# A hybrid trunk step: the work between the RWKV scans in three strips, moved between engines, and begun earlier

## The reference

```
def centred_shift(p, mu_prev, mu_next):
    ...
    return p + mu_prev * (p_prev - p) + mu_next * (p_next - p)

kkf = heads((k * k_k).astype(jnp.float32))
kk = kkf * lax.rsqrt(jnp.sum(kkf * kkf, axis=-1, keepdims=True) + 1e-12)
g = jax.nn.sigmoid(glo) @ g_up
for d, rev in enumerate((False, True)):
    w_log = -softplus(-(w0[d] + tanh(wlo) @ w_up[d])) - 0.5
    decay = exp(-exp(w_log))
    a = sigmoid(a0[d] + alo @ a_up[d])
    kd = k * (1 + (a - 1) * k_a)
    y, s_fin = rwkv_scan(r, decay, kd, v, kk, a, s0[:, d], rev)
    ...
yf = ys[0] + ys[1]
mu = mean(yf); var = mean(square(yf - mu))          # over the 64 of a head
y = (yf - mu) * rsqrt(var + GN_EPS) * gn_g + gn_b
y = y + (bonuses[0] + bonuses[1]) * v
return y * g, finals
```

## Time and profile before

| what | us |
|---|---|
| median of 3 runs | 3958.61 |
| lowest, highest | 3956.07, 3959.44 |
| the profiled execution | 3956.13 |
| its span | 3954.4 |
| TensorE busy in it | 3578.8 (91%) |
| VectorE busy in it | 1311.3 (33%) |
| mean granted TensorE clock | 0.953 |

### The profile page before, as it was taken

One profiled execution on the slowest core, in us unless ns is written; L12 is line 12 of the kernel. 1 busy time (PEld: TensorE's weight loads), 2 busy tenths in 40 slices (PEclk: granted clock), 3 DMA queues, 4 the chain that ended last, 5 costly groups with the idle time before them and its releaser, 6 DMA issues. The chain is left out here.

```text
span 3954.4 us, 81654 instructions
## 1 busy us (share of the span) xinstructions
PE 3578.8 (91%) x36990; PEld 3118.8 (79%) x36990; DVE 1311.3 (33%) x3130; ACT 650.1 (16%) x1649; POOL 189.7 (5%) x150
## 2 busy tenths in 40 slices
PE   5979798897979988739999999999999999999995
PEld 2467494775935554439999999999999999999995
DVE  3476777767634443451111111111111111111112
ACT  2222323222214452200000000000000000000001
POOL 0000101001010000000000000000000000000000
PEclk7989899998989989869999999999999999999997
DMA  7200000000031103149878787877878787878772
GB/s 315 59 8 12 12 4 20 3 16 12 4 89 30 30 2 112 70 149 347 267 262 268 261 273 264 268 264 267 270 267 267 266 271 261 269 262 268 262 262 107
DMA packets 498248, 664.33 MB, mean 168 GB/s; under 512 B 31134, under 2 KB 436950, under 8 KB 494830
## 3 DMA queue, kind: packets, MB, share of 16 engines
q1 hardware_dynamic: 492094, 640.18, 48.3%
q0 software_dynamic: 5632, 18.88, 1.8%
q10 hardware_dynamic: 176, 0.05, 0.0%
HBM read 630.70 MB, written 28.36 MB: 167 GB/s over the span
## 5 line engine op out<-in xcount | busy, mean ns | idle before, releaser
L1990 PE MATMUL bank<-e_hid,e_wd 128*128 128x144 f32 x5632 | 760.1, 288 | 0.0
L1978 PE MATMUL bank<-e_xT,e_wg 128*128 128x144 f32 x5632 | 749.5, 286 | 1.0 <-ACT e_xT L2032 1.0
L1978 PE MATMUL bank<-e_xT,e_wu 128*128 128x144 f32 x5632 | 748.2, 286 | 0.0
L2075 DVE TENSOR_TENSOR e_tm<-bank,e_sg 128x144 f32<-128x144 f32 x352 | 108.4, 308 | 1852.9 <-ACT e_sg L2039 1852.9
L1978 PEld LDWEIGHTS bank<-e_xT,e_wg 128*128 128x128 f32 x5632 | 715.5, 190 | 1.0 <-issue 1.0
L1990 PEld LDWEIGHTS bank<-e_hid,e_wd 128*128 128x128 f32 x5632 | 710.5, 190 | 5.6
L1978 PEld LDWEIGHTS bank<-e_xT,e_wu 128*128 128x128 f32 x5632 | 714.5, 190 | 0.0
L2039 ACT ACTIVATE e_sg<-bank 128x144 f32<-128x144 f32 x352 | 102.5, 291 | 1998.2 <-PE bank L1978 1998.2
L519 PE MATMUL bank<-hT_x,wblk 128*128 128x512 f32 (+1 forms) x672 | 237.2, 512 | 10.0 <-DMA wblk<-in_w_in 8.6
L519 PEld LDWEIGHTS bank<-hT_x,wblk 128*128 128x128 f32 x672 | 115.6, 199 | 125.0 <-issue 113.3
L661 PE MATMUL bank<-r_TW,r_X 64*64 64x64 f32 x2880 | 167.6, 220 | 4.3 <-DVE r_X L1073 1.3
(11 more groups left out here) (314 smaller groups left out, 3518.5 us busy)
## 6 DMA issues: line engine op xcount, KB each, us to landing
e_wg<-in_e_gate SPq DMA_DIRECT2D x176, 1024.0 KB
e_wu<-in_e_up SPq DMA_DIRECT2D x176, 1024.0 KB
e_wd<-in_e_down SPq DMA_DIRECT2D x176, 1024.0 KB
h_wmod<-in_w_mod SPq DMA_DIRECT2D x24, 1024.0 KB, 18.3
wblk<-in_w_in SPq DMA_DIRECT2D x22, 512.0 KB
h_x<-in_x_sample SPq DMA_DIRECT2D x8, 512.0 KB, 7.5
wo<-in_w_out SPq DMA_DIRECT2D x2, 2048.0 KB, 11.3
o_x<-in_x_sample SPq DMA_DIRECT2D x8, 512.0 KB
```

Source lines behind the costliest of these rows:

```text
L1978: last = nc.tensor.matmul(bank[6 + b % 2][:, j * TOK:(j + 1) * TOK], w[s][:, k, f], xT[e % 2][:, k, :], start=(k == 0), stop=(k == KD - 1))
L1990: last = nc.tensor.matmul(bank[k // PER_BANK][:, c:c + TOK], wd[s][:, b % DUO, k * P:(k + 1) * P], hid[:, b % 2, :], start=(b == 0 and k % ...
L2075: V.tensor_tensor(tm[b % 2][:, :], bank[6 + b % 2][:, 0:TOK], sg[b % 2][:, :], ALU.mult)\
```

## The change

- Head sums of k's norm and of the variance are taken in three strips: `head_sums` writes the sum of each third of the tokens (384) to 32 partitions, 16 for each head, so the root and the reciprocal run on 96 x 384 (tile rs) instead of 128 x 1152. `heads_back` multiplies the strips by selT (rows of `head_ones`, scaled by 1/16) and so brings them to all 128 partitions in PSUM, from where VectorE uses them directly.
- ScalarE writes the scaled copy (the shift's first term) from PSUM beside the raw copy, piece by piece as the projection ends (`block_piece`); VectorE keeps the two fused steps (`neighbours`). ScalarE also squares k for the norm.
- The reverse direction's sum is formed from the forward scan by one subtraction and one addition instead of a subtraction, an addition and a second subtraction from the middle.
- The finish of a pair is cut into `finish_first`, `finish_var` and `finish_back` on TensorE, and stands inside the next pair's list: the gates and the projection of k are issued between its steps. pv and pc have two buffers, the output gate has a tile of its own (`gate`), and `constants` for the next pair is computed inside the finish on VectorE.
- r's projection and the gates of the second direction are reordered; v's later pieces stand behind the output gate; the shift of v stands behind prep_ok, and v_major waits for it. SyncE issues the next pair's weights after the output gate's product of this pair, before the scan.
- The block for GpSimd is not in the diff: its four products and one sum per pair, and what they wait for by name, are as before.

The diff, cut to its core:

```diff
+                def head_sums(rhs, b):
+                    for j in range(3):
+                        last = nc.tensor.matmul(bank[b][32 * j:32 * (j + 1), 0:THIRD], K.head_ones[:, HN - DUP:HN + DUP],
+                                                rhs[:, j * THIRD:(j + 1) * THIRD], start=True, stop=True)
+                    return last
+                def heads_back(first):
+                    for j in range(3):
+                        rows = slice(32 * j, 32 * (j + 1))
+                        last = nc.tensor.matmul(bank[first + j][:, 0:THIRD], selT[rows, :], rs[rows, :],
+                                                start=True, stop=True)
+                    return last
...
+                def finish_first(p):
+                    pe.wait_ge(s_ok, p * (STEPS + 1) + STEPS + 1)
+                    for d in range(2):
+                        for hs in HS:
+                            last = nc.tensor.matmul(bank[6][hs, d * HN:(d + 1) * HN], S[hs, d, :], K.idc[hs, :],
+                                                    start=True, stop=True)
+                    last.then_inc(st_t, 1)
+                    pe.wait_ge(tw_ok, p * (GR * NTW) + GR * NTW)
+                    pe.wait_ge(kv_ok, p * GR + GR)
+                    pe.wait_ge(bonus_in, p + 1)
+                    pe.wait_ge(o_ok, p * STEPS + STEPS)
+                    full(K.head_ones[:, :], aa, 3).then_inc(bonus_ps, 1)
+                    pe.wait_ge(y_sum, p + 1)
+                    full(K.head_ones[:, :], t0, 0).then_inc(mean_ps, 1)
+                    pe.wait_ge(bonus_ok, p + 1)
+                def finish_var(p):
+                    pe.wait_ge(sqd, p + 1)
+                    head_sums(t1, 0).then_inc(var_ps, 1)
+                def finish_back(p):
+                    pe.wait_ge(rs_ok, p + 1)
+                    heads_back(0).then_inc(back_ps, 1)
                 for p in range(PAIRS):
+                    if p:
+                        finish_first(p - 1)
+                        pe.wait_ge(st_out, p)
                     pe.wait_ge(up_in, p * 80 + 80)
                     gates(0, slice(0, HN)).then_inc(wg_ps, 1)
+                    pe.wait_ge(w_in[0], p * 32 + 32)
+                    project(0, 3, pieces=[0], chunks=range(0, 4))
+                    if p:
+                        finish_var(p - 1)
+                    project(0, 3, pieces=[0], chunks=range(4, KD))
                     project(0, 3, pieces=[1])
-                    pe.wait_ge(root_ok, p + 1)
-                    pe.wait_ge(w_in[1], p * 16 + 32)
-                    project(1, 0, pieces=[0])
+                    if p:
+                        finish_back(p - 1)
                     pe.wait_ge(wg_ok, p * 2 + 1)
                     project(0, 3, pieces=[2])
                     pe.wait_ge(rawd, p * 3 + 3)
                     gates(0, slice(HN, P)).then_inc(ag_ps, 1)
-                    project(1, 0, pieces=[1, 2])
+                    pe.wait_ge(pair_ok, p + 1)
+                    pe.wait_ge(w_in[1], p * 16 + 32)
+                    project(1, 0, pieces=[0])
 
                     pe.wait_ge(sq_ok, p + 1)
+                    head_sums(kk, 3).then_inc(norm_ps, 1)
                     pe.wait_ge(ag_ok, p * 2 + 1)
-                    full(K.head_ones[:, :], t0, 3).then_inc(norm_ps, 1)
-                    pe.wait_ge(norm_ok, p + 1)
                     gates(1, slice(0, HN)).then_inc(wg_ps, 1)
+                    project(1, 0, pieces=[1])
+                    pe.wait_ge(nrs_ok, p + 1)
+                    pe.wait_ge(wg_ok, p * 2 + 2)
+                    heads_back(3).then_inc(nback_ps, 1)
+                    project(1, 0, pieces=[2])
+                    pe.wait_ge(kk_ok, p + 1)
+                    gates(1, slice(HN, P)).then_inc(ag_ps, 1)
                     pe.wait_ge(rawd, p * 3 + 4)
                     pe.wait_ge(w_in[0], p * 32 + 48)
                     project(0, 0, pieces=[0])
-                    pe.wait_ge(wg_ok, p * 2 + 2)
-                    gates(1, slice(HN, P)).then_inc(ag_ps, 1)
-                    project(0, 0, pieces=[1, 2])
                     pe.wait_ge(ag_ok, p * 2 + 2)
                     full(gup[:, :], sigg, 3).then_inc(gate_ps, 1)
                     pe.wait_ge(st_in, p * 32 + 32)
@@ -573,6 +638,7 @@
                             last = nc.tensor.matmul(bank[6][hs, d * HN:(d + 1) * HN], ST[hs, d, :], K.idc[hs, :],
                                                     start=True, stop=True)
                     last.then_inc(st_t, 1)
+                    project(0, 0, pieces=[1, 2])
...
+                    pe.wait_ge(shifted, p * 3 + 6)
...
+                def finish(p):
+                    act.wait_ge(centred, p + 1)
+                    nc.scalar.activation(t1[:, :], t0[:, :], ACT.Square).then_inc(sqd, 1)
+                    act.wait_ge(var_ps, p + 1)
+                    nc.scalar.activation(rs[0:96, :], bank[0][0:96, 0:THIRD], ACT.Sqrt, bias=K.eps[0:96, 2:3],
+                                         scale=1.0 / HN).then_inc(root_ok, 1)
                 for p in range(PAIRS):
-                    def block_raw(i):
-                        act.wait_ge(proj, p * 3 + (3 + i))
-                        act.wait_ge(shifted, p * 3 + (3 + i))
-                        copy_raw(0 if i else 3)
+                    pv, pc = pv2[p % 2], pc2[p % 2]
+                    def block_piece(i, c):
+                        first, out, j = (3, 0, 0)[i], (k, r, v)[i], ORDER[i]
+                        at, m = PIECES[c]
+                        if c == 0:
+                            act.wait_ge(shifted, p * 3 + (3 + i))
+                        act.wait_ge(piece_ok, 3 * (p * 3 + 2 + i) + c + 1)
+                        nc.scalar.activation(out[:, at:at + m], bank[first + c][:, 0:m], ACT.Copy, scale=pc[:, j:j + 1])
+                        dst = at + SAMPLE if at < NS else PROMPT
+                        last = nc.scalar.activation(raw[:, dst:dst + m], bank[first + c][:, 0:m], ACT.Copy)
+                        if c == 2:
+                            last.then_inc(rawd, 1)
 
                     def decays(d):
 
@@ -836,35 +900,43 @@
                         nc.scalar.activation(e12[:, d, :], mid[:, d, 1, :], ACT.Exp,
                                              scale=-DECAY).then_inc(exps_ok, 1)
 
-                    act.wait_ge(pair_ok, p + 1)
+                    if p:
+                        finish(p - 1)
                     act.wait_ge(pv_ok, p + 1)
                     act.wait_ge(wg_ps, p * 2 + 1)
                     gates(sig, bias=pv[:, 6:7]).then_inc(wg_ok, 1)
-                    block_raw(0)
+                    for c in range(3):
+                        block_piece(0, c)
                     act.wait_ge(ag_ps, p * 2 + 1)
                     gates(aa, bias=pv[:, 8:9]).then_inc(ag_ok, 1)
-                    decays(0)
-
+                    act.wait_ge(pair_ok, p + 1)
                     act.wait_ge(ag_ok, p * 2 + 1)
                     nc.scalar.activation(kds[:, :], aa[:, :], ACT.Identity, scale=pv[:, 11:12],
                                          bias=pc[:, 3:4]).then_inc(aff_ok, 1)
-                    block_raw(1)
+                    decays(0)
+                    act.wait_ge(shifted, p * 3 + 4)
+                    nc.scalar.activation(kk[:, :], k[:, :], ACT.Square, scale=pv[:, 10:11]).then_inc(sq_ok, 1)
                     act.wait_ge(norm_ps, p + 1)
-                    full(t1, 3, ACT.Sqrt, bias=K.eps[:, 1:2]).then_inc(norm_ok, 1)
+                    nc.scalar.activation(rs[0:96, :], bank[3][0:96, 0:THIRD], ACT.Sqrt, bias=K.eps[0:96, 1:2])\
+                      .then_inc(nroot_ok, 1)
                     act.wait_ge(wg_ps, p * 2 + 2)
                     gates(sig, bias=pv[:, 7:8]).then_inc(wg_ok, 1)
+                    block_piece(1, 0)
+                    block_piece(1, 1)
+                    decays(1)
+                    block_piece(1, 2)
                     act.wait_ge(aa_used, p * 2 + 1)
                     act.wait_ge(ag_ps, p * 2 + 2)
                     act.wait_ge(aff_ok, p * 2 + 1)
                     gates(aa, bias=pv[:, 9:10]).then_inc(ag_ok, 1)
-                    decays(1)
-                    block_raw(2)
+                    block_piece(2, 0)
                     act.wait_ge(aa_used, p * 2 + 2)
                     nc.scalar.activation(aa[:, :], aa[:, :], ACT.Identity, scale=pv[:, 11:12],
                                          bias=pc[:, 3:4]).then_inc(aff_ok, 1)
-
                     act.wait_ge(gate_ps, p + 1)
-                    full(sig, 3, ACT.Copy).then_inc(gate_ok, 1)
+                    full(gate, 3, ACT.Copy).then_inc(gate_ok, 1)
+                    block_piece(2, 1)
+                    block_piece(2, 2)
...
+                def finish(p):
+                    pv = pv2[p % 2]
+                    dve.wait_ge(st_t, p * 2 + 2)
+                    V.tensor_copy(ST[:, :, :].rearrange("p d n -> p (d n)"), bank[6][:, 0:P]).then_inc(st_out, 1)
```

(66 more changed lines are left out.)

170 lines of the change are left out of this document (76 added, 94 removed).

## The result

The changed kernel takes 3863.82 us (median of 4 runs, 3860.96 to 3867.98) beside 3957.34 for the kernel before (4 runs, 3954.26 to 3959.44). The ratio is 0.9765, interval 0.9748 to 0.9782. The forecast was 3864, with a range of 3848 to 3890. The profiled execution took 3860.96; forecast was 3861.

A forecast was written before the change was run, and what follows sets the result against it. VectorE's chain between scans was taken as the bound, TensorE's afterwards. Savings of 70.8 (three pairs), 15.3 (pair 0) and 9.0 (last finish) sum to 95 of 3956.1, giving 3861; the median lies 2.5 higher, so 3864, range 3848 to 3890.

The forecast's parts named there:

- pair 0, first T earlier: Preparation before the first scan: M at 209.1 instead of 224.4, 15.3 saved; T is a pair's last state transpose.
- three pairs: Three gaps between scans, each 73.3 instead of 96.9 us including the scan's start cost: 70.8 saved.
- last finish: After the last scan, from T to yA: shorter variance strips, root and reciprocal save 9.0 us, counted in full.
- The chain on TensorE: TensorE's ordered work and waits in pair 1's gap put M 70.5 us after T, before clock cost.
- T to M: The gap, from a pair's last state transpose to the next pair's first M product; forecast near 73 us.
- Its two waits: TensorE in the gap: 1.9 us before the norm strips, 1.4 us after the second a gates, both behind ScalarE.
- The prediction's own sign of being wrong: In the gap: a TensorE wait over 3 us, strips of 2 us, or half clock over more than a few us.
- The rival with strips in turn: Strip products run one after another, not abreast: 1.2 us more each, 19 in all, 3883 us; 13 in 100.
- The clock term: TensorE at 1.2 GHz after short waits in each gap: between 0 and 3.4 us lost, 1.7 taken.
- The start of the scan: v's shift, held behind GpSimd's key sum, delays the inverse from 6.4 to 7.5 us after M: 1.1 lost.
- yA: VectorE's end of the previous pair's finish, forecast at 392.3, before the a gates at 393.9.
- The slower side: TensorE stays at 1.2 GHz through the gap: 40 us longer than before per gap, 4080 us; 2 in 100.

The follow-up runs named there:

- finish_first: The changed kernel with the next pair's gates and k's second piece only after the last pair's strips are back, sigmoid and first sum only after yA; 3861.28 us.
- idle_filled: The changed kernel with throwaway matmuls on TensorE before its waits for the square of k and for r's last scaled copy; 3862.72 us, ratio 0.9766.
- scale_dve: The changed kernel with the first step of the shift of k, r and v on VectorE again; 3879.89 us, ratio 0.9805.
- gate_late: The changed kernel reordered on several engines to fill TensorE's waits in the gap, with the output gate's product behind v's second piece; 3856.05 us.

## Why the prediction was right, point by point

The sum by its own terms, in the profiled executions:

| term | forecast | measured | from |
|---|---|---|---|
| pair 0, first T earlier | 15.3 | 13.2 | 367.44 - 354.28 |
| three pairs | 70.8 | 69.0 | 720.16 - 651.13 |
| last finish | 9.0 | 8.5 | 25.38 - 16.89, T to yA's end |
| behind the mixer | 0 | 4.5 | 2842.8 - 2838.3, last yA to the end |
| sum | 95 | 95.2 | 3954.4 - 3859.2 |

**The mixer gave 90.7, not 95.** That the total was met so closely is partly luck. The 4.5 behind the mixer are not the change's: that code is the same, and over the 14 profiles this part varies by 8 us. In the attention one stretch of 20 us, for one, ran at a clock of 0.67 before and 0.90 after (that the 4.5 come from it is not shown); busy time by stretch, before, then after:

```profile
1454.50:1474.50 20.00, 14.58 (x98) 9.89 (x96) 9.46 (x28) 9.76 (x18) 0.00 (x0) 0.67 0.00 1
```
```profile
1363.80:1383.80 20.00, 13.44 (x110) 9.15 (x108) 10.61 (x31) 11.15 (x21) 0.00 (x0) 0.90 0.00 0
```

**In the three pairs two errors offset each other.** The 69.03 are 67.68 from the gaps (289.97 us in all before, 222.29 after) and 1.35 from the scans. The forecast's 70.8 were 74.1 from the gaps, three times 96.9 less 72.2, and 3.3 lost in the scans. So the gaps gave 6.4 less and the scans 4.7 more than forecast, which is luck again.

**The chain on TensorE was right.** Forecast 70.5 and 1.7 for the clock, 72.2 from T to M; measured 75.2, 73.55, 73.55. The base of 96.9 was 0.3 too long: it took the first scan's 143.1 for all four, and the three gaps had 96.7 on average. Its two waits, 1.9 and 1.4, were 1.94 and 1.50. TensorE's busy time of 70.3 in the first gap is the forecast's 67 and 3.4 of lost clock. The rest of T to M, 1.3 a gap, are small prices added up, as 7.0 instead of 6.9 for a piece and 0.83 instead of 0.6 for the last copy. The prediction's own sign of being wrong, half clock over more than a few us, came in the first gap (6.8 us of it), and it is there that the gap is 3 us over the forecast's 72.2.

**The strips were right:** 0.85 and 0.92 for 0.8, the reciprocal 2.55 for 2.45. The rival with strips in turn is out.

**The clock term had the right size per wait and the wrong count.** Of the two waits, none or one or both were followed by half clock: in the first gap it is the one of 1.94 (3.83 and 8.85 instead of 2.20 and 7.13, 3.4 in all), in the second only the one of 1.50 (8.83, 1.7), in one gap of finish_first both. All slow rows of the gap follow idle time, and filling it took them all away. Forecast was 1.7 in every gap; 3.4, 1.7 and 1.7 came.

**The start of the scan was mis-sized, and helped.** The forecast added 1.1 to every pair, the inverse starting 7.5 us after M instead of 6.4. With v's step held it starts 7.34 after M, without 5.74 (5.8 by the forecast's own lower bound): both values were right. Two things were not. The step was held in two pairs of four, at 1.6 each. And 6.4 is the smallest of the four starts of before (6.43 to 7.11): there TensorE came to M at half clock, for a time that differed from pair to pair (0.69 us for the row that takes 0.44 now; v_major's 72 products took 2.50 to 3.18 and take 2.31 now). So an unheld scan is 142.4 and a held one 144.0, where the four of before had 143.1 to 143.7. The Trainium skill (SBUF — State Buffer, SBUF: two separate sides) has a VectorE instruction with two SBUF inputs wait out a GpSimd one that began first; the trace agrees, 3.15 where the key sum had begun and 1.55 where it had ended. What I missed is that the hold and the clock are not two costs to be added: idle_filled took 6.7 us from the gaps, and the scans took all of it back, by the hold and by half clock behind it.

**Pair 0** gave 2.1 less. The three transfers of the selection matrix were taken as 0 (bounds 0 to 1). They stood 22.5 us in SyncE's queue, behind the spread of the bias table, and the weights stood behind them. Timelines of SyncE and TensorE, kernel after:

```profile
109.26 22.53 SPq L488 DMA_DIRECT2D r_selT<-head_ones  x3
```
```profile
137.44 4.17 PE L540 MATMUL bank<-r_lora,r_wup 64*128 64x512 f32 x6 [13.74 <-DMA r_gup<-in_g_up]
...
172.09 3.11 PE L540 MATMUL bank<-r_lora,r_wup 64*128 64x512 f32 x6
175.12 9.57 PE L532 MATMUL bank<-hT_x,wblk 128*128 128x512 f32 x16
```

The gates began at 137.44 instead of 136.89, 0.55 later, but that is not the price of the transfers: with the same transfers they began at 136.79 in scale_dve and at up to 140.58 in others. From the issue of the spread to the gates are 27.5 us before and 27.7 to 29.6 in the twelve profiles with the transfers in which TensorE begins with the gates, so the transfers may have cost 0.2 to 2.1; with one profile of the kernel before it stays open. The other 1.6 are the clock behind the wait for the square of k (3.11 and 9.57, 3.3 lost where 1.7 was taken). **The last finish** gave 0.5 less, since both strip products ran at half clock there, the one back with 1.66:

```profile
1012.88 1.50 PE L553 MATMUL bank<-r_t,head_ones 128*32 128x384 f32 x6 [2.94 <-ACT r_t L872]
...
1017.71 1.66 PE L561 MATMUL bank<-r_rs,r_selT 32*128 32x384 f32 x6 [3.33 <-DVE r_rs L1083]
```

**yA** ended at 379.69, 1.7 us before the a gates did (forecast 1.6). The slower side, half clock through the gap, did not come; what speaks against it stands: in the gaps of the kernel after the clock was at half for 3.4 or 6.8 us, and the most in any gap with TensorE as its bound was 13.7 (finish_first, its gap of 78.1).

Open: what the three transfers cost pair 0; why the same wait of 1.50 is followed by half clock in one gap and not in another, and what in the attention's 20 us differs from execution to execution; none of them was tried.

## What to carry to other kernels

Work out the path, not the busy time: of two reciprocals made shorter by the same 4.8 us, one was worth nothing inside the loop and the other 5 to 6 a gap, as TensorE waited for what stood behind it and its clock fell behind the waits. When an engine that was hidden becomes the bound, fill its waits with its own later work, but look at what its earlier end then meets: here 6.7 us won on TensorE were handed back by a GpSimd sum that held one VectorE step, and by half clock behind that hold. A GpSimd instruction whose result is needed late belongs where VectorE's path does not pass, or on VectorE in an idle stretch: that alone took a pair from 215.0 (gate_late) to 212.2.

## What the runs showed of the hardware that was not expected

Three DMA issues of a 32-row tile stood 22.53 us in SyncE's queue behind a transfer that spreads a table, where single issues beside them take 0.4 to 0.6. Half clock after idle time is not certain at these lengths: waits of 1.50, 1.94 and 2.60 were followed by it in some pairs and not in others (the 2.60 for v not in the first two scans of the kernel after, but in three of four in idle_filled), those of 2.45, 2.57, 3.33, 3.43, 4.26 and 4.36 wherever they stood in the mixer. With two fillers of 512 columns, 1.88 us of throwaway work, in the one wait and two of 512 and 256 in the other, the clock was 1.00 over all three gaps.
